# Second layer's queries, keys and values projected with channels on partitions, and VectorE's steps of the first layer's block inverse put in TensorE's order

## The reference

```python
q, k, v, z = jnp.split(x @ w_in, [SWA_Q, SWA_Q + SWA_KV, SWA_Q + 2 * SWA_KV], axis=-1)
x1, x2 = xf[..., :half], xf[..., half:]          # half = 32 of a head's 64 channels
rope = jnp.concatenate([x1 * cos - x2 * sin, x2 * cos + x1 * sin], axis=-1)
s = einsum(q, k) * HD ** -0.5;  p = softmax over the window's keys and the sink;  o = p @ v
out = (o * silu(z)) @ w_out
```

## Time and profile before

| | |
|---|---|
| median of 3 runs | 985.26 us (984.84 to 986.24) |
| the profiled execution | 985.34 us, its span 983.5 us (1.84 us lie outside of the span) |
| TensorE's granted clock | 0.998 of full speed |
| PE busy | 957.8 us, 97% of the span |
| DVE, ACT, POOL busy | 643.0, 452.1, 314.2 us |
| chain that ended last | 82% PE, 8% DVE, 6% ACT |

### The profile page before, as it was taken

One profiled execution on the slowest core, in us unless ns is written; L12 is line 12 of the kernel. 1 busy time (PEld: TensorE's weight loads), 2 busy tenths in 40 slices (PEclk: granted clock), 3 DMA queues, 4 the chain that ended last, 5 costly groups with the idle time before them and its releaser, 6 DMA issues.

```text
span 983.5 us, 19957 instructions
## 1 busy us (share of the span) xinstructions
PE 957.8 (97%) x7678; PEld 788.1 (80%) x7678; DVE 643.0 (65%) x1212; ACT 452.1 (46%) x1310; POOL 314.2 (32%) x635
## 2 busy tenths in 40 slices
PE   7999999999999899999999999999999999999997
PEld 6888788787878687888788888888787777778885
DVE  4576868676777768574546666753443677789575
ACT  5655557566666565664455211230213555556000
POOL 1008474755565564746100000010010535440000
PEclk9999999999999999999999999999999999999999
DMA  6233322414142415131301522130303201013211
GB/s 219 66 77 101 87 81 55 113 37 128 37 113 55 113 32 133 29 103 48 113 22 51 175 75 65 45 95 1 97 22 65 67 24 46 24 67 112 82 65 64
DMA packets 95181, 73.80 MB, mean 75 GB/s; under 512 B 32848, under 2 KB 84208, under 8 KB 95088
## 3 DMA queue, kind: packets, MB, share of 16 engines
q1 hardware_dynamic: 60768, 55.69, 19.2%
q10 hardware_dynamic: 34320, 16.84, 6.8%
HBM read 61.47 MB, written 11.04 MB: 74 GB/s over the span
## 4 chain that ended last, share of the span: by engine, by line
PE 82%; DVE 8%; ACT 6%; issue 2%; DMA 1%; POOL 0%; ACTq 0%; DVEq 0%; POOLq 0%
PE ps L800 28%; PE ps L989 15%; PE ps L1172 9%; PE ps L1061 9%; PE ps L1002 2%; DVE tok L1596 2%; PE ps L1194 2%; PE ps L1137 2%; PE ps L959 2%; DMA ws_raw<-in_b_w_in 1%; PE ps L970 1%; PE ps L968 1%; PE ps L877 1%; PE ps L947 1%; PE ps L946 1%
## 5 line engine op out<-in xcount | busy, mean ns | idle before, releaser
L800 PE MATMUL ps<-act_hi,w_hi 128*128 128x512 f32 x512 | 223.7, 437 | 0.1
L800 PE MATMUL ps<-act_hi,w_lo 128*128 128x512 f32 x512 | 201.1, 393 | 0.0
L800 PE MATMUL ps<-act_lo,w_hi 128*128 128x512 f32 x512 | 200.1, 391 | 0.0
L1596 DVE SCALAR_TENSOR_TENSOR tok<-xs,convw,tok 128x512 f32<-128x512 f32 x144 | 115.3, 801 | 15.5 <-ACT xs L1295 13.7
L713 POOL TENSOR_TENSOR rank<-inverse,tok 128x60 f32<-128x60 f32 (+24 forms) x248 | 94.3, 380 | 97.6 <-DMA tok<-blocks_in 79.4
L800 PEld LDWEIGHTS ps<-act_hi,w_lo 128*128 128x128 f32 x512 | 96.1, 188 | 21.3
L800 PEld LDWEIGHTS ps<-act_hi,w_hi 128*128 128x128 f32 x512 | 97.0, 189 | 12.0 <-issue 0.3
L716 POOL TENSOR_TENSOR inverse<-inverse,rank 128x60 f32<-128x60 f32 (+24 forms) x248 | 100.2, 404 | 19.4
L800 PEld LDWEIGHTS ps<-act_lo,w_hi 128*128 128x128 f32 x512 | 97.2, 190 | 10.1
L989 PE MATMUL ps<-wo_lo,act_hi 128*128 128x512 f32 x224 | 87.4, 390 | 0.1
L989 PE MATMUL ps<-wo_hi,act_hi 128*128 128x512 f32 x210 | 82.5, 393 | 0.2 <-DVE act_lo L1688 0.2
(11 more groups left out here) (268 smaller groups left out, 2088.1 us busy)
## 6 DMA issues: line engine op xcount, KB each, us to landing
w_raw<-in_a_w_in ACTq DMA_DIRECT2D x32, 512.0 KB, 4.2
tok<-in_x SPq DMA_DIRECT2D x8, 512.0 KB, 7.1
decay<-gc_rows SPq DMA_DIRECT2D x8, 512.0 KB, 5.0
tok<-blocks_in SPq DMA_DIRECT2D x32, 128.0 KB, 2.6
v_turn<-v_tok SPq DMA_DIRECT2D x8, 512.0 KB, 5.8
v_tok<-v_turn SPq DMA_DIRECT2D x32, 128.0 KB, 2.9
xres<-in_x SPq DMA_DIRECT2D x8, 512.0 KB, 3.4
ws_raw<-in_b_w_in SPq DMA_DIRECT2D x16, 256.0 KB, 2.7
```

The lines of the kernel that those rows point to most:

```text
L800: mm = pe.matmul(ps[:, g % 2, :], lhs[:, k, :], rhs[:, k, HALF * b:HALF * (b + 1)], start=(i == 0), stop=(i == GROUP - 1))
L1596: ins = dve.scalar_tensor_tensor(conv[b], xs[:, b, k:k + HALF], convw[:, k, tile:tile + 1], conv[b], ALU.mult, ALU.add)
```

## The change

Layer 1's queries, keys and values are projected the other way around: the weights are stationary (128 channels), the activations move (512 tokens). There are 20 groups of 24 matmuls of 512 columns: n = 0 and 2 keys, n = 1 and 3 values, n = 4..19 queries (8 channel tiles by 2 halves of the tokens). Queries and keys need no transposes then. The rotary tables do, once (`turn_tables`, 8 transposes), and so do the values (`turn_values`, 8). The rotary embedding needs each half of a head beside the other: ACT copies the four 32-partition quarters of a group across (`swap_halves`), and DVE multiplies and adds (`rotate`), into bT or kd directly; for keys it also copies each head's rows to the other 64 partitions. Queries use three PSUM banks in turn instead of four. The pair that frees slices is n = 10 and 11, and ACT and DVE both take slices 9 to 15 ahead of n = 10. The loads of v_rows wait for the last rotation. The table load for Exp is no longer asked for in advance.

In layer 0, DVE's step X makes the two transposes that level 0 reads first and signals after them, and writes the memset for heads 0 and 6 only (the others find the zeros of an earlier head); of the three copies after level 1 the one that level 2 reads comes first and has its own signal, and level 3 waits for the other two (s_xd).

```diff
-TOKEN_BANKS = (0, 1, 6, 7)
+KV_GROUPS = 4
+QK_GROUPS = KV_GROUPS + 2 * NK
+ROPES = QK_GROUPS - 2
+GROUP_BANKS = [2, 3, 6, 7] + [5 + n % 3 for n in range(KV_GROUPS, QK_GROUPS)]
...
 FIRST = 2 * GROUP + 7 * STEP
-GATE_FROM = 18
+GATE_FROM = 13
 GATE_SPLIT = 10
-EARLY_LOGITS = 20
...
-    if n < 2:
...
-    return range(WR, SLICES) if n == refill else ()
+    if n == KV_GROUPS:
+        return (WR - 1,)
+    return range(WR, SLICES) if n == REFILL_AT else ()
+
+
+def is_value(n):
+
+    return n < KV_GROUPS and n % 2 == 1
+
+
+def rope_of(n):
+
+    return n // 2 if n < KV_GROUPS else n - 2
+
+
+def tile_of(n):
+
...
-            sp.dma_start(sinr[:, :, :], rope_sin.rearrange("(t p) d -> p t d", p=P)).then_inc(q_small, 16)
+            sp.dma_start(vv[:, :, 0:HD], rope_cos.rearrange("(t p) d -> p t d", p=P)).then_inc(q_small, 16)
+            sp.dma_start(vv[:, :, HD:P], rope_sin.rearrange("(t p) d -> p t d", p=P)).then_inc(q_small, 16)
...
-            sp.wait_ge(q_val, NT)
+            sp.wait_ge(q_val, 2)
...
-                    sp.wait_ge(q_group, 3 * NT)
+                    sp.wait_ge(q_rope, ROPES)
...
@@ -913,6 +948,7 @@
                 elif i == 2:
                     pe.wait_ge(s_xl, 2 * h + 1)
                 else:
+                    pe.wait_ge(s_xd, h + 1)
                     pe.wait_ge(s_ut, 2 * h + 2)
...
-                hi, lo = (kv_hi[:, k, :], kv_lo[:, k, :]) if bl == 0 else (ws_hi[:, sl, :], ws_lo[:, sl, :])
+                bank = ps[:, GROUP_BANKS[n], :]
+                if n < KV_GROUPS:
+                    b = n // 2
+                    cols = slice(P * (n % 2), P * (n % 2 + 1))
+                    hi, lo = kv_hi[:, k, cols], kv_lo[:, k, cols]
+                else:
+                    tile, b = tile_of(n)
+                    sl = (NK * (tile // 4) + k) % WR
+                    cols = slice(P * (tile % 4), P * (tile % 4 + 1))
+                    hi, lo = ws_hi[:, sl, cols], ws_lo[:, sl, cols]
...
+                    if n == 0:
+                        pe.wait_ge(L[0]["yev"], 2 * (NT - 1))
...
+                        pe.wait_ge(L[0]["xlo"], NT)
+                    elif n == 2:
+                        pe.wait_ge(L[0]["xlo"], 2 * NT)
+                    elif n == KV_GROUPS:
+                        pe.wait_ge(q_rope, 2)
+                    elif n == KV_GROUPS + 1:
+                        pe.wait_ge(q_vch, 2)
+                    elif n >= KV_GROUPS + 3:
+                        pe.wait_ge(q_rope, rope_of(n - 3) + 1)
+                if n >= KV_GROUPS and (n - KV_GROUPS) % NK == 0:
+                    pe.wait_ge(q_lo, NK * (tile // 4) + k + 1)
...
+                    lhs = (hi, hi, lo)[j]
+                    rhs = (act_hi, act_lo, act_hi)[j]
+                    mm = pe.matmul(bank, lhs, rhs[:, k, HALF * b:HALF * (b + 1)],
...
+            def turn_tables():
+                pe.wait_ge(q_small, 48)
+                pe.wait_ge(L[0]["yev"], 2 * NT)
+                for t in range(NT):
+                    mm = pe.transpose(ps[:, t // 4, (t % 4) * P:(t % 4 + 1) * P], vv[:, t, :], ident[:, :])
+                mm.then_inc(q_ttr, 1)
...
+                    project_channels(0)
                     turn(NT - 1)
+                    turn_tables()
+                    project_channels(1)
...
+            def turn_values(b):
+                pe.wait_ge(q_vch, b + 1)
+                if b == 0:
+                    pe.wait_ge(q_cos, 1)
+                    pe.wait_ge(q_sin, 1)
+                for c in range(4):
+                    mm = pe.transpose(ps[:, b, c * P:(c + 1) * P], vv[:, 4 + c, :], ident[:, :])
                 mm.then_inc(q_tr, 1)
...
+            last = KV_GROUPS + NK - 1
+            for n in range(2, QK_GROUPS):
...
+                    project_channels(n)
+                if n in (2, KV_GROUPS):
+                    turn_values(n // 2 - 1)
+                if n == FIRST_LOGITS[0]:
                     pe.wait_ge(q_c, 17)
-                    pe.wait_ge(q_tev, 2 * NT)
+                    pe.wait_ge(q_rope, rope_of(last) + 1)
+                    pe.wait_ge(q_val, 2)
                     logits(0)
+                elif n == FIRST_LOGITS[1]:
+                    logits(1)
...
-            pe.wait_ge(q_tev, 3 * NT - 3)
-            logits(1)
-            turn_tokens(3 * NT - 2)
-            project_gate(0, 0)
-            turn_tokens(3 * NT - 1)
-            project_gate(0, 1)
-            project_gate(0, 2)
+            for third in range(3):
+                project_gate(0, third)
+            pe.wait_ge(q_rope, ROPES)
             logits(2)
             logits(3)
-            pe.wait_ge(q_tev, 3 * NT)
...
+            def swap_halves(n):
+                r = rope_of(n)
+                act.wait_ge(q_group, n + 1)
+                if r >= 2:
+                    act.wait_ge(q_rope, r - 1)
+                for a in range(0, P, 32):
+                    b = a + 32 - 2 * (a % 64)
+                    ins = act.activation(other_half(r)[a:a + 32], ps[b:b + 32, GROUP_BANKS[n], :], ACT.Copy,
+                                         scale=SCALE if n >= KV_GROUPS else 1.0)
+                ins.then_inc(q_swap, 1)
...
+            act.wait_ge(q_ttr, 1)
+            for b in range(2):
+                for e in range(2):
+                    ins = act.activation(cosr[64 * e:64 * e + 64, HALF * b:HALF * (b + 1)], ps[0:64, b, :], ACT.Copy)
+            ins.then_inc(q_cos, 1)
+            for n in range(QK_GROUPS):
...
-                if bl == 0:
-                    act.wait_ge(q_rope, n + 1)
...
+                if is_value(n):
+                    act.wait_ge(q_group, n + 1)
+                    if n == 3:
+                        act.wait_ge(q_tr, 1)
+                    act.activation(vv[:, 4:8, :].rearrange("p a b -> p (a b)"), ps[:, GROUP_BANKS[n], :], ACT.Copy)\
+                       .then_inc(q_vch, 1)
+                else:
+                    swap_halves(n)
+                if n in (2, KV_GROUPS):
+                    b = n // 2 - 1
+                    act.wait_ge(q_tr, b + 1)
+                    act.activation(vv[:, 4 * b:4 * b + 4, :].rearrange("p a b -> p (a b)"), ps[:, b, :], ACT.Copy)\
+                       .then_inc(q_val, 1)
+                if n == FIRST_EXPONENTIALS[0]:
+                    act.wait_ge(q_rope, 10)
+                    act.wait_ge(s_vd, 16)
                     exponentials(0)
...
+                elif n == FIRST_EXPONENTIALS[1]:
+                    exponentials(1)
...
                     x = xT[r % 2]
-                    dve.memset(xr[r][0:32, :, 32:64], 0.0)
                     dve.transpose(xr[r][0:32, :, 0:32], x[0:32, :, 0:32])
+                    dve.transpose(xr[r][64:96, :, 0:32], x[64:96, :, 64:96]).then_inc(s_xr, 1)
+                    if r in (0, 6):
+                        dve.memset(xr[r][0:32, :, 32:64], 0.0)
                     dve.transpose(xr[r][32:64, :, 32:64], x[32:64, :, 32:64])
-                    dve.transpose(xr[r][64:96, :, 0:32], x[64:96, :, 64:96]).then_inc(s_xr, 1)
                 elif kind == "L" and b == 1:
                     x = xT[r % 2]
                     dve.wait_ge(s_lv, 4 * r + 2)
                     src = ps[:, 6, 0:256].rearrange("p (c j) -> p c j", c=NT)
-                    dve.tensor_copy(x[0:32, :, 32:64], src[0:32])
+                    dve.tensor_copy(xr[r][32:64, :, 0:32], src[32:64]).then_inc(s_xl, 1)
                     dve.tensor_copy(x[64:96, :, 96:128], src[64:96])
-                    dve.tensor_copy(xr[r][32:64, :, 0:32], src[32:64]).then_inc(s_xl, 1)
+                    dve.tensor_copy(x[0:32, :, 32:64], src[0:32]).then_inc(s_xd, 1)
                 elif kind == "L" and b == 3:
                     dve.wait_ge(s_lv, 4 * r + 4)
                     for odd in range(2):
...
+            def rotate(n):
+                r = rope_of(n)
+                dve.wait_ge(q_swap, r + 1)
+                other = other_half(r)
+                if n < KV_GROUPS:
+                    b = n // 2
+                    cut = slice(HALF * b, HALF * (b + 1))
+                    own.next(dve.tensor_tensor(other, other, sinr[:, cut], ALU.mult))
+                    keys = slice(P + HALF * b, P + HALF * (b + 1))
+                    for c in range(KVH):
+                        rows = slice(64 * c, 64 * c + 64)
+                        own.next(dve.tensor_tensor(kd[rows, c, keys], ps[rows, GROUP_BANKS[n], :], cosr[rows, cut],
+                                                   ALU.mult))
+                    own.wait()
+                    for c in range(KVH):
+                        rows = slice(64 * c, 64 * c + 64)
+                        own.next(dve.tensor_tensor(kd[rows, c, keys], kd[rows, c, keys], other[rows], ALU.add))
+                    own.wait()
+                    for c in range(KVH):
+                        ins = dve.tensor_copy(kd[64 - 64 * c:128 - 64 * c, c, keys], kd[64 * c:64 * c + 64, c, keys])
+                    ins.then_inc(q_rope, 1)
+                else:
```

(54 more changed lines are left out.)

111 lines of the change are left out of this document (17 added, 94 removed).

## The result

The changed kernel takes 996.56 us as the median of 4 executions (991.95 to 999.84), the kernel before 985.05 beside it (984.68 to 986.24): a ratio of 1.0104, 95% interval 1.0081 to 1.0127. It is slower by 11.5 us, outside of the range 980.5 to 988.5. The profiled execution took 997.26 us, span 995.5.

A forecast was written before the change was run, and what follows sets the result against it. PE was taken as the bound, busy 957.8 of 983.5 us with 82% of the chain. From the profiled 985.34, +0.5 for the projection and -1.2 for the block inverse gave 984.6 us, no tellable change; range 980.5 to 988.5.

The forecast's parts named there:

- The first layer-1 wait: Before group 4 of layer 1's projection: PE waits for the second key rotation, a hole of 5.2 us.
- The second pair: Before group 13: PE waits for late slice 15, then group 10's swap and rotation, a hole of 5.8 us.
- the walk: Layer 1's projection stepped through in the new queue order, asking at each wait what comes last: this half costs 0.5 us.
- the first rival: Layer 1's swaps and rotations: ACT and DVE overlap on part tiles too, giving 981.7 us; chance 0.24.
- the refill rival: Slices 9 to 15: three DMA round trips at 3.9 us each add 2.7 us, giving 987.3; chance 0.14.
- The prediction's sensitivities: Changes of the whole time: part-tile overlap -2.9, matmuls +1.5, key copies +1.0, slice landing -0.8 or +1.5, inverse -0.7 to +1.2.
- Matmul distance: Layer 1's groups from 5 on: matmuls 0.2275 us apart instead of 0.233, 5.46 a group, about 2 us gained.
- v_rows: Before `values`: loads issued after the last rotation land 10.9 us later, leaving PE a hole of 2.7 us.
- the forecast's case: Whole kernel: within 2 us of no change, range 983.3 to 987.2 us; chance 0.38.
- three holes: Layer 1's PE waits before group 4, before group 13 and before `values`: 5.2, 5.8 and 2.7, together 13.7 us.
- The block inverse: Layer 0's heads: earlier releases of levels 0 and 2 gain 1.7 us worked out, 1.2 booked, bounds 0 and 1.9.
- The third rival: Layer 1's projection: the holes are not there and only the removed transposes show, 975 us; no separate chance given.

The follow-up runs named there:

- e3: The changed kernel with 63 matmuls, results unread, added where PE waits (head 0, groups 4, 12, 13, v_rows): 987.95 us, ratio 1.0015.
- e6: The changed kernel with five PSUM banks in turn instead of three for groups 4 to 13: 984.76 us, ratio 0.9988.
- e2: The changed kernel with the block inverse of the kernel before, so the projection change alone: 995.21 us, ratio 1.0092.
- e5: The changed kernel with v_rows read back before the last rotation has ended: 988.20 us, ratio 1.0029.
- e10: The changed kernel with unread matmuls added ahead of groups 4, 12 (last step) and 13 alone; head 0 and v_rows waits open: 993.31 us, ratio 1.0062.
- e4: The changed kernel with the old inverse, five banks, slices 4 to 7 and 9 to 15 earlier, v_rows earlier: 973.03 us, ratio 0.9858.
- e8: e4 with the inverse's change and 2 + 6 unread matmuls filling head 0's waits: 972.22 us, ratio 0.9869.
- e1: The kernel before with the block inverse's change alone: 984.29 us, ratio 0.9974.
- e7: e4 with the block inverse's change, so both parts of the change plus the four edits: 975.00 us, ratio 0.9886.

## Why the prediction was wrong, point by point

- **The first layer-1 wait** was to be 5.2 us, released by a DVE copy into kd: it was 5.2, released by L2012. The chain to it is the one that was walked, slices 4 and 5 ahead of the swap. **The second pair** was to be 5.8, late slice 15 first: 1.7 + 2.8 = 4.5; PE came there later than walked, since the clock had fallen in between. At full clock the walk holds: the gate groups were to start at 754.1, 219.5 after layer 0's output started; in e3 it is 219.3.
- **Prices.** A swap copy starts the next after 0.60 (0.61 taken), so there is no overlap, and VectorE's operations on 64 partitions don't overlap either (L2004 starts at 646.69 and 647.41, each about 0.7 long): the first rival is out. The Trainium skill's 93 ns of overlap (ScalarE: Activation LUTs, "What ACT_TABLE_LOAD costs"), stated behind durations for tiles of 128 partitions, does not hold for copies of 32 partitions in this trace. A key copy from SBUF to SBUF took 0.42 (0.45 taken) where a tensor_tensor of the same tile, also from SBUF, took 0.70. The Trainium skill (VectorE: DVE Perf Modes, "Mode 2×_2P") gives a float32 copy from SBUF two results a cycle and a tensor_tensor in float32 one, and these two rows agree. The three slices of the refill on the chain landed in 2.60 to 2.86, far below the 3.9 a trip from which the refill rival decides; it is out as well. The prediction's sensitivities, all at their high ends, add up to 984.6 + 5.2 = 989.8 and not to 989; that changes nothing here.
- **Matmul distance** was to be 0.2275 from group 5 on. It is 0.2292 in groups 5 to 9 (27.50 / 120) and 0.2321 later (16.71 / 72). What counts is the 7 groups behind the second pair of waits, 0.11 us each: 0.8 more than summed, given back by a refill that ended earlier than walked.
- **v_rows** was to land 10.9 after the issue: 12.0 in the changed kernel, 13.7 in e3. The wait, at full clock, is 5.5 us instead of 2.7. This term was mis-sized by 2.8. A part of it is a reading: the prediction took the time at which the traffic of before had ended, 764.9. The last of the four loads was issued at 756.01 and landed 9.8 later (the line below, kernel before), at 765.8, which is 11.8 after the first issue, and the changed kernel's 12.0 is near that. So 0.9 of the 2.8 was there to be read. The other 1.9 is the slower landing in e3, which e6 has as well; what slowed it was not found.

```profile
DMA to landing us min/median/max: 4.6/7.6/9.8
```

  With it the sum for layer 1 is 0.5 + 2.8 = 3.3, which is what e3 leaves at full clock. e3's ratio is 1.0015, no change that can be told: without the falls the change is the forecast's case.
- **The step that failed** is the one that set each hole's price to its length: "Against 9.4 us of transposes and their waits, 2 us from closer matmuls and small pieces stand three holes, 13.7 us together." The prediction never spoke of the granted clock, though holes of that length were new to this stage. In the traces each of the three places is followed by matmuls at 0.50 where the wait is left open (changed, e2, and those left open in e5 and e10), and none of them is where it is gone or filled to the end (e4, and the first two in e3 and e10). In the profiled execution layer 1 lost 8.4 us, against 3.3 at full clock. The stretched pieces give this difference of 5.1 nearly: 8.21 - 5.60 = 2.6 in group 4, 14.04 - 11.20 = 2.8 in the 48 matmuls behind 719, some 1.6 behind v_rows (1.1 of it again in the `logits`); less 1.7, by which the wait for v_rows was shorter here than in e3: 5.3.
- **The block inverse** gave what was said: PE's waits for the head's chain (those for DVE and ACT from 100 to 540) fell from 7.4 us to 5.6, L921's from 2.4 to 0.8 (1.3 predicted), and layer 0's output starts 1.9 us earlier in e3, where the clock doesn't fall in layer 0, than before (532.71 against 534.65). 1.2 were booked, 1.7 worked out. In the changed kernel's profile this gain is buried under head 0's fall: 538.32 - 532.71 = 5.6 us.
- The third rival, 975 without holes, was 2 to 3 us too dear: e4, with the inverse of before, is at 973.0 and e8 at 972.2.

The sum of the profiled execution: layer 0: -1.9 by the inverse and +5.6 by a fall in head 0 that e2 and e4 show with the first layer of before as well; layer 1: +3.3 by waits and +5.1 by falls, of which the trace of the kernel before has none. Together 12.1, of 11.9 measured between the two profiled executions. Against the forecast of 984.6 the profiled execution is 12.7 too long: 10.7 is clock (5.6 + 5.1), which had no term in the sum, 2.8 is v_rows, and 0.7 goes the other way, since the inverse gave 1.9 and not 1.2. That the slow executions of the kernel before, at a clock of 0.991, also fell in head 0 is likely but not shown: its one trace has no fall there.

## What to carry to other kernels

Price a wait of TensorE twice: by its length, and by what the granted clock takes from the matmuls behind it; where a change gathers small holes into a few long ones, look at this second price first. Count banks and queue order before the form of the work: the same projection, with the same inverse, was 9 us slower than before with three banks in turn and late reads (e2), and 13 us faster with five and early ones (e4). Read a transfer's end from its landing, and not from the moment at which the traffic thins out. When executions of one kernel lie at two levels, compare their granted clocks before explaining a part of the difference by the change.

## What the runs showed of the hardware

- The clock has two levels in these rows, 0.50 and 1.00, and values in between are stretches that hold both. The Trainium skill (TensorE: Matmul & The Clock Gate, "Part 1: The HAM clock gate") has the lower level as the array's default that activity releases; e3 and e10 agree, where activity with useless operands kept it up.
- A fall costs more than a reader of PE's busy row would think: 5.4 us behind the first three waits of 9.7 us together. In head 0, two waits of 0.6 and 1.5 us (changed, e1, e5, e6, e7, e10) or 1.2 and 0.7 (before, e2, e4) were followed by over 12 us at the lower level in some profiled executions (changed, e2, e10), by some 10 in e6, 7 in e7 and under 4 in e4, and by none in the others. What decides between them for the same instructions was not found.
- The same four v_rows loads took, the slowest of each kernel, 9.8 us from issue to landing in the kernel before, 10.2 in e4 and 11.6 in e3 and in e6, with the same bytes.
